# Gate/up products of an expert's back token groups interleaved with those of its front rows, in three variants by token count

## The reference

```python
h = _rmsnorm(x, norm2_w).reshape(B * S, D)
top_vals, top_idx = lax.top_k(logits, TOP_K)        # 4 of 32 experts for each token
gu = xb @ w_gate_up[e] + b_gate_up[e]               # 1024 -> 2 * 1024
g = jnp.minimum(gu[:, :D_FF], SWIGLU_LIMIT)
u = jnp.clip(gu[:, D_FF:], -SWIGLU_LIMIT, SWIGLU_LIMIT)
act = (u + 1) * g * jax.nn.sigmoid(SWIGLU_ALPHA * g)
return act @ w_down[e] + b_down[e]                  # 1024 -> 1024
```

## Time and profile before

| | |
|---|---|
| median of 3 runs | 1733.96 us |
| profiled execution: its time | 1735.41 us |
| profiled execution: its span | 1733.7 us |
| TensorE (PE) busy | 1474.0 us, 85% |
| weight loads of TensorE (PEld) | 595.0 us, 34% |
| VectorE (DVE) busy | 782.4 us, 45% |
| ScalarE (ACT) busy | 356.0 us, 21% |
| GpSimd (POOL) busy | 96.7 us, 6% |
| moved by DMA | 598.10 MB, 345 GB/s on average |
| mean granted clock of TensorE | 0.903 |

### The profile page before, as it was taken

One profiled execution on the slowest core, in us unless ns is written; L12 is line 12 of the kernel. 1 busy time (PEld: TensorE's weight loads), 2 busy tenths in 40 slices (PEclk: granted clock), 3 DMA queues, 4 the chain that ended last, 5 costly groups with the idle time before them and its releaser, 6 DMA issues.

```text
span 1733.7 us, 32093 instructions
## 1 busy us (share of the span) xinstructions
PE 1474.0 (85%) x11950; PEld 595.0 (34%) x11951; DVE 782.4 (45%) x1160; ACT 356.0 (21%) x822; POOL 96.7 (6%) x173
## 2 busy tenths in 40 slices
PE   3868887779788978899998998999899999899970
PEld 2433333346433354332332332333233332232320
DVE  2789879997786335221332232132132131131326
ACT  3212212222222111111211211212112122121220
POOL 0000010000000000000100000000000000000000
PEclk8989995679898857999999999999899999999995
DMA  9557888988998785598999999999999999999986
GB/s 327 182 187 258 283 295 272 331 279 292 311 301 270 242 352 207 227 392 339 429 420 403 427 417 396 412 418 411 392 421 412 401 428 411 397 428 399 428 351 253
DMA packets 127292, 598.10 MB, mean 345 GB/s; under 512 B 20503, under 2 KB 20517, under 8 KB 102026
## 3 DMA queue, kind: packets, MB, share of 16 engines
q1 hardware_dynamic: 109088, 560.20, 81.9%
q10 hardware_dynamic: 8634, 20.00, 3.4%
q0 software_dynamic: 9504, 17.06, 2.6%
HBM read 589.36 MB, written 25.87 MB: 355 GB/s over the span
## 4 chain that ended last, share of the span: by engine, by line
PE 40%; DMA 19%; DVE 2%; issue 1%; ACT 0%; DVEq 0%; SPq 0%; ACTq 0%
PE bank L1511 25%; DMA wts<-in_w_gate_up 16%; PE bank L1548 8%; PE bank L1530 4%; DMA wts<-in_w_down 3%; PE bank L1501 1%; PE bank L1618 1%; DVE v_ring L2139 1%; PE bank L1559 1%; PE bank L1599 0%; DVE q_b L2139 0%; DMA h_tok<-h_rows,v_tok 0%; ACT k_T L1155 0%; DVEq L2127 0%; ACT k_T L1138 0%
## 5 line engine op out<-in xcount | busy, mean ns | idle before, releaser
L1511 PE MATMUL bank<-wts,h_T 128*32 128x512 f32 x4032 | 443.9, 597 | 9.7 <-DMA wts<-in_w_gate_up 5.2
L2061 DVE TENSOR_SCALAR q_T<-bank 128x512 f32<-128x512 f32 x32 | 22.1, 692 | 636.9 <-PE bank L1511 636.9
L1511 PEld LDWEIGHTS bank<-wts,h_T 128*32 128x32 f32 x4032 | 129.5, 111 | 308.3 <-issue 296.4
L1548 PE MATMUL bank<-wts,k_T 128*32 128x512 f32 x2048 | 228.3, 597 | 8.0 <-issue 4.9
L1530 PE MATMUL bank<-wts,h_T 128*32 128x512 f32 x992 | 132.6, 675 | 52.2 <-DMA wts<-in_w_gate_up 50.4
L1658 DVE TENSOR_TENSOR wts<-wts,q_b 128x1024 f32<-128x1024 f32 x128 | 158.1, 1235 | 23.1 <-DMA wts<-in_cache_k 17.4
L1661 DVE TENSOR_REDUCE sc<-wts 128x16 f32<-128x1024 f32 x128 | 156.2, 1220 | 4.4
L1145 ACT ACTIVATE h_T<-bank 128x512 f32<-128x512 f32 x66 | 35.9, 595 | 573.5 <-PE bank L1501 573.5
L1548 PEld LDWEIGHTS bank<-wts,k_T 128*32 128x32 f32 x2048 | 64.9, 110 | 149.0 <-issue 139.5
L1223 PE MATMUL bank<-wts,h_T 128*8 128x128 f32 (+1 forms) x480 | 92.7, 465 | 12.3 <-ACT h_T L854 6.4
L1155 ACT ACTIVATE k_T<-bank 32x256 f32<-32x256 f32 x256 | 95.7, 374 | 13.6 <-PE bank L1548 10.2
(11 more groups left out here) (330 smaller groups left out, 1375.8 us busy)
## 6 DMA issues: line engine op xcount, KB each, us to landing
wts<-in_w_gate_up SPq DMA_DIRECT2D x126, 2048.0 KB, 15.8
wts<-in_w_down SPq DMA_DIRECT2D x64, 2048.0 KB, 18.3
wts<-in_cache_k SPq DMA_DIRECT2D x256, 256.0 KB, 3.7
v_ring<-in_cache_v SPq DMA_DIRECT2D x160, 256.0 KB, 3.8
wts<-in_cache_v SPq DMA_DIRECT2D x96, 256.0 KB, 3.9
wts<-in_w_in SPq DMA_DIRECT2D x5, 2048.0 KB, 24.1
wts<-y_rows SPq DMA_DIRECT2D x4, 2048.0 KB, 15.1
wts<-in_w_out ACTq DMA_DIRECT2D x8, 512.0 KB, 6.2
```

What stands on the lines that cost most here:

```text
L1511: m = nc.tensor.matmul(PS[part][p0:p0 + 32, :], lhs[:, 32 * b:32 * b + 32], rhs[:, part * F + half * 512:part * F + half * 512 + 512], sta ...
L1548: m = nc.tensor.matmul(PS[4][p0:p0 + 32, :], act_T[0][:, k, a0:a0 + 32], chunk[c][:, k, n * 512:(n + 1) * 512], start=(c == 0 and k == 0), ...
```

## The change

The back products of an expert's groups are done in the same pass over the chunks as the front products. `gate_up(i, backs)` replaces `gate_up_front` and `gate_up_back`: for each chunk and k block it does the 4 products of each back group (`backs` of them) and then the 8 front products; `w_used[c]` is incremented once, after the chunk. The bias products of the back groups and of the front rows follow at the end. `down(i, backs)` puts `down_back` and `down_front` into one function with the order of products as before: all back passes, then the front pass.

`by_size` has three variants of each product function written out, with 2, 1 and 0 back groups, and branches to one of them. So the code of each place (gate/up and down of the written-out experts, of the loop, of the end and of the overflow body) has the front products three times and the back products of one group three times, where before it had the front products once and those of a back group twice. The number of products that are executed stays the same.

```diff
-            def gate_up_front(i, chunk=gu_chunk):
+            def gate_up(i, backs, chunk=gu_chunk):
...
                 for c in range(4):
                     pe.wait_ge(w_full[c], i * 16 + 16)
                     for k in range(2):
-                        products(hg_T[:, 2 * c + k, :], chunk[c][:, k, :], c == 0 and k == 0, False)
+                        for b in range(backs):
+                            back(b, hg_T[:, 2 * c + k, :], chunk[c][:, k, :], c == 0 and k == 0, False)
+                        m = front(hg_T[:, 2 * c + k, :], chunk[c][:, k, :], c == 0 and k == 0, False)
+                    m.then_inc(w_used[c], 1)
                 pe.wait_ge(sel_done, i + 1)
-                products(sel[0:96, :], b_split[0:96, :], False, True)
+                for b in range(backs):
+                    back(b, sel[0:96, :], b_split[0:96, :], False, True)
+                front(sel[0:96, :], b_split[0:96, :], False, True).then_inc(gu_done, 1)
...
-            def down_front(i, chunk=dn_chunk, full=w_full[4:6], loads=0):
+            def down(i, backs, chunk=dn_chunk, full=w_full[4:6], loads=0):
+                for b in range(backs):
+                    for c in range(2):
...
-            def by_size(front, back, i, size=None):
+            def by_size(products, i, size=None):
 
                 if size is None:
                     size = pe.value_load(n_tok[0:1, bass.ds(i, 1)], min_val=0, max_val=CAP)
                 with pe.If(size > 64):
-                    back(i, 0)
                     with pe.If(size > 96):
-                        back(i, 1)
-                front(i)
+                        products(i, 2)
+                    with pe.If(size < 97):
+                        products(i, 1)
+                with pe.If(size < 65):
+                    products(i, 0)
                 return size
```

More of the change, by code:

```diff
@@ L1502, in transpose_x, with front @@
                     m.then_inc(xt_full, 1)
-            def gate_up_front(i, chunk=gu_chunk):
-                def products(lhs, rhs, start, stop):
+            def gate_up(i, backs, chunk=gu_chunk):
+                def front(lhs, rhs, start, stop):
                     for part in range(2):
@@ L1514, in products, with back @@
                     return m
[L1516 to L1526, removed]
+                def back(b, lhs, rhs, start, stop):
                     for part in range(2):
@@ L1536, in gate_up_back @@
                     for k in range(2):
-                        products(hg_T[:, 2 * c + k, :], chunk[c][:, k, :], c == 0 and k == 0, False)
+                        for b in range(backs):
+                            back(b, hg_T[:, 2 * c + k, :], chunk[c][:, k, :], c == 0 and k == 0, False)
+                        m = front(hg_T[:, 2 * c + k, :], chunk[c][:, k, :], c == 0 and k == 0, False)
+                    m.then_inc(w_used[c], 1)
                 pe.wait_ge(sel_done, i + 1)
-                products(sel[0:96, :], b_split[0:96, :], False, True)
-            def down_front(i, chunk=dn_chunk, full=w_full[4:6], loads=0):
+                for b in range(backs):
[4 more added lines that the diff above has]
+                    for c in range(2):
+                        pe.wait_ge(full[c], i * 16 + 16 * (loads + 1))
+                        for k in range(4):
+                            a0 = 64 * b + 32 * c
+                            for q in range(4):
+                                nc.tensor.matmul(PS[5][32 * q:32 * q + 32, 256 * b:256 * (b + 1)],
+                                                 act_T[1][:, k, a0:a0 + 32], chunk[c][:, k, q * 256:(q + 1) * 256],
+                                                 start=(c == 0 and k == 0), stop=(c == 1 and k == 3))
                 for c in range(2):
@@ L1551, in down_front, with first_gate_up, last_down, late_down @@
                     m.then_inc(w_used[4 + c], 1)
[L1553 to L1579, removed]
-            def by_size(front, back, i, size=None):
+            def first_gate_up(i, backs):
+                gate_up(i, backs, first_gu)
+            def last_down(_i, backs):
+                down(0, backs, last_dn, last_full)
+            def late_down(i, backs):
+                down(i, backs, loads=-1)
+            def by_size(products, i, size=None):
                 if size is None:
@@ L1601, in enter_late, with expert_block @@
                 m.then_inc(late_summed, 1)
-            def expert_block(i, before=None, front=gate_up_front, back=gate_up_back):
+            def expert_block(i, before=None, products=gate_up):
                 after(pe, gclip_done, i * 2)
                 pe.wait_ge(xt_copied, i * 2 + 2)
-                size = by_size(front, back, i)
+                size = by_size(products, i)
                 transpose_x(i + 1)
@@ L1621, in expert_block, with down_block @@
                 return size
-            def down_block(i, first, front=down_front, back=down_back, size=None):
+            def down_block(i, first, products=down, size=None):
                 pe.wait_ge(at_copied, i * 2 + 2)
@@ L1627, in down_block @@
                     pe.wait_ge(y_back, i)
-                by_size(front, back, i, size)
+                by_size(products, i, size)
             pe.wait_ge(order_done, 1)
@@ L1637, in _ @@
             pe.wait_ge(meta_out, 2)
-            expert_block(1, 0, first_gate_up_front, first_gate_up_back)
+            expert_block(1, 0, first_gate_up)
             with pe.Fori(2, E) as i:
                 expert_block(i, i - 1)
-            down_block(E - 1, False, last_down_front, last_down_back)
+            down_block(E - 1, False, last_down)
             pe.wait_ge(meta_out, 3)
@@ L1646, in _ @@
                     size = expert_block(j + E)
-                    down_block(j + E, False, late_down_front, late_down_back, size)
+                    down_block(j + E, False, late_down, size)
         @block.vector
```

## The result

The changed kernel takes 2119.85 us (median of 4 runs, 2103.86 to 2131.34), the kernel before 1731.58 us in 4 runs (1728.41 to 1736.56). The ratio is 1.2233, with a 95% interval from 1.2141 to 1.2324: slower by 388 us. The forecast was 1901 us with a range up to 1990. The direction was right and the mechanism too; the size (+167 us) was less than half of what came.

The account below looks back on a forecast made before the run. The DMA was taken to bound the loop (floor 907 us, PE 856); 243 us of stands lift PE to 1099, loop +152, plus 11 and 4.4 outside: +167 on 1735.41 gives 1903, stated as 1901 us, range 1712 to 1990.

Parts of the forecast that it names:

- What bounds the kernel: Loop over experts: DMA is the bound, floor 907 us at 427 GB/s against 947.1 measured; PE needs 856.
- Part 1, -33 us: Interleaved pass in the loop: earlier slot release wins 33 of 40 us of unused DMA time, between 0 and -40.
- first visits: First runs of code not loaded yet: +11 us ahead of the loop; some +6 in it if code is held.
- the rival with no gain: Loop: code held, interleaving gains nothing, only first visits count: 1757 us; chance 0.05.
- the held case: Loop: new code still held, -33 us there, less than offset by first visits and jumps: 1723 us; chance 0.23.
- Part 2, the mechanism: Three variants in the loop: code outgrows what is held, PE stands for loads, waits for chunks vanish; loop +152 us.
- Part 2, the count of stands: Far jumps in the loop: 3 stands of PE for code a pair of experts, 45 in 15 pairs; bounds 0 to 7.
- Part 2, the price of one: One stand in the loop: 4.4 us plus 1.0 for the slow clock behind it, 5.4 us; bounds 3 and 6.3.
- Outside the loop, +11 and +4.4: Jumps over variants on first visits in experts 0 and 1 (+11 us) and in the last down product (+4.4 us).

Follow-up runs that it names:

- e5: The down product interleaved as well, branches inside each chunk and one copy of the code, against e1: 1724.71 us, ratio 0.9957.
- e11: e5 without three quarters of the down product's front products (output not the reference's): 1715.54 us, ratio 0.9888.
- e1: Against the changed kernel: gate/up interleaved in one code copy, branches inside each chunk, down product as in the kernel before: 1727.93 us, ratio 0.9982.
- e3: Against the changed kernel: down product with one copy of its code, gate/up still in three variants: 1750.37 us, ratio 1.0111.
- e2: Against the changed kernel: three written-out variants kept, but in gate/up all back products before the front products: 2126.78 us, ratio 1.2292.
- e14: e3 plus 62 products that never run ahead of expert 1, so the loop begins a whole block further on: 1751.8 us.
- e12: The kernel before plus 266 products in the loop's body that never run but stay in the code: 1752.6 and 1782.9 us.
- e13: e3 plus 28 products that never run ahead of expert 1, so the loop begins half a block further on: 1799.2 and 1905.2 us.
- e6: Against the changed kernel: down product's code with its back groups once and the front twice (1811 instructions): 1909 and 1959 us.
- e7: Against the changed kernel: down product's code with three back groups and the front twice (1942 instructions): 1900.8 and 1922.8 us.
- e8: The changed kernel with its variants ordered none, one, two back groups, the rare one last: 1938.98 us, ratio 1.1201.

## Why the prediction was right in direction and wrong in size

**What bounds the kernel.** Half right. The DMA bounds the loop, but its floor was taken from one undisturbed window of 34 us (427 GB/s). No run here holds that rate over the loop: e5 and e11 show 412 to 413 GB/s at a share of 1.00 over 600 us. By that the floor of the loop is 947.1 x 409/413 = 938 us, not 907. Over the longer stretch from 770 to 1650 us both show 416, against 410 in the kernel before, which would make it 933.

**Part 1, -33 us.** Wrong in size. The earlier release gives 3 us in the loop with gate/up alone (e1: 944.0) and 7 with both products (e5: 1724.71 in all). Of the 40 us that I saw as unused, some 9 to 14 were there. A wait was also handed on: from the gate/up back pass to the down back pass. The prediction named only PE or the transfers' rate as the next in line. For held code with first visits, which is e3 (1750.37), the rival with no gain (1757, its chance was 0.05) was nearer than the held case as I priced it (1723).

**Part 2, the mechanism.** Right. Code is loaded again in each round, TensorE stands for it with nothing else to wait for, the waits for weights vanish, and the DMA falls from the bound. e2 shows it without the order of the change, e1 the order without the copies.

**Part 2, the count of stands.** This is the step that failed: "I take 3, since the old body is known to fit". I counted the jump back twice and one more. The profile shows four in a pair (5.91, 4.46 and two in the 10.06), and in five pairs a fifth, before the down front products (4.2 to 4.3 us). I had also taken 15 pairs; the loop has 13 large experts, so fewer pairs and four small experts more. The 45 were to be 61: 16 jumps back to a small expert, 13 before a down back pass, 12 stretches with two in a row, the five, and three behind the gate/up products of the expert with more than 96 tokens (8.6 us, counted as two, and 2.8). (The other 12 stretches, of 1.1 us on average, stand a few products behind the double ones; I count them with those.) The bounds that I gave, 0 to 7 a pair, hold.

**Part 2, the price of one.** Mis-sized as well: 4.4 + 1.0 = 5.4 us. The stands of the loop are 322.8 us, and the slow clock behind them takes 987.8 - 856 = 132 us more. With 61 stands that is 5.3 + 2.2 = 7.5 us each, beyond my upper bound of 6.3. Single stands in the loop last 4.2 to 6.8 us (and the 2.8), most of them more than the 4.39 that I had read in the earlier trace rows; why they are longer is not shown. And I had halved the cost of the slow clock, where it is paid in full: 16.11 against 14.17, and 6.49 against 3.6. Count and price multiply: 45 x 5.4 = 243, and 61 x 7.5 = some 455. The loop was to go from 947 to 1099 us, and went to 1311.

**Outside the loop, +11 and +4.4.** The right size. First visits ahead of the loop cost 4.70, 3.48 and 1.25 us in the chain of the kernel after, and the loop's entry comes at 742.4 us instead of 729.3 (13 us later). The last down product waits 8.44 us and not 4.92, so 3.5 us.

**How much code is held.** The Trainium skill ("Runtime: NRT & Kernel Launch", section "Instruction fetch mechanics") gives TensorE 2048 instructions in blocks of 256. The runs agree with eight blocks, if one counts those that a pair touches, each with the one behind it. By the listing that is 6 in the kernel before, 5 in e1 and e5, 8 in e3, e14 and e12: held (e12 nearly). It is 9 in e13, e6 and e7, 10 in e2, e8 and the changed kernel: not held. That the block behind counts is my reading and not shown: without it the same runs have 4 to 6 blocks where the code is held and 7 or 8 where it is not, which parts them as well. The section's sentence on only two lines does not agree with the runs: e3 goes through six blocks in each pair and runs 750 us without a load.

What stays open: which block is dropped when there is no room, and so why ten blocks give four stands a pair in one order of the code and three in another, and nine give one in e13 and more in e6 and e7.

## What to carry to other kernels

Count the code of a loop's body before a branch is turned into written-out variants, and place the branch around as few products as possible: a branch around one chunk's products cost nothing that e1 shows, the copies cost 388 us. A profile in which neither the engine nor the DMA is full, with "issue" at the same instructions in each round, calls for a look at the code queue's packets. And a rate seen in a short window is no floor for a loop; to know the limit of the transfers, take compute away and see whether the rate rises.

## What the runs showed of the hardware that I had not expected

The place of a loop in its 16 KB block can decide over 47 us: e13 (1799.2) differs from e14 (1751.8) only by 34 products ahead of the loop that never run. A stand of TensorE of 4 to 7 us is followed by a granted clock of 0.55 or so on what comes next (in the pair above 4 us of the front pass and the whole back pass), so that it costs 7.5 us on average and not 5.3. And the DMA share is 1.00 or 1.01 at rates from 404 to 430 GB/s in windows of 20 us (e11, 1000 to 1080), so a share of 1.00 does not fix the rate:

```profile
1000.00:1020.00 20.00, 15.16 (x164) 6.53 (x157) 5.91 (x9) 2.23 (x4) 1.23 (x2) 1.00 1.01 426
1020.00:1040.00 20.00, 18.24 (x180) 6.33 (x175) 2.50 (x5) 4.08 (x10) 1.19 (x2) 1.00 1.00 404
1040.00:1060.00 20.00, 15.86 (x124) 6.19 (x120) 8.41 (x13) 6.41 (x14) 1.23 (x2) 0.83 1.00 406
1060.00:1080.00 20.00, 16.03 (x162) 6.33 (x158) 2.46 (x4) 1.60 (x3) 1.38 (x3) 1.00 1.01 430
```
